# The second output projection in seven products for each pair of token tiles, with the sums on GpSimd

## The reference, cut to what matters

```
mixed = concat([norm(att) * g_att, norm_per_head(mlstm * sigmoid(gate)) * g_ml])   # [1024, 1024]
x     = x1 + mixed @ w_out_2          # second output projection, the product that is changed
q     = (rms_norm(x) * norm_cross_2) @ w_cq_2       # queries of the attention to memory
mem   = rms_norm(mem_2) * norm_mem_2                # its keys and values come from mem
```

## Time and profile before

| what | value |
|---|---|
| median of three runs | 2126.6 us (2122.72 to 2126.88) |
| span of the profiled execution | 2124.1 us |
| PE busy in it | 2037.9 us (96%) |
| DVE, ACT, POOL busy | 915.3, 573.6, 326.1 us |
| first turn of the phase to the `MANY` products of the next projection | 1165.49 to 1300.31 us of the span |
| PE busy in that stretch | 134.48 of 134.82 us |
| DVE, ACT, POOL busy in that stretch | 64.65, 31.86, 8.60 us |

### The profile page before, as it was taken

How to read it: one execution, slowest core, us unless ns; L and a number is a source line. 1 busy time by engine, 2 the same in 40 slices (tenths; PEclk the granted TensorE clock), 3 DMA queues, 4 the chain that set the end, 5 groups by cost and what they waited for, 6 DMA issues and landing times.

```text
span 2124.1 us, 37932 instructions
## 1 busy us (share of the span) xinstructions
PE 2037.9 (96%) x15636; PEld 1158.4 (55%) x15636; DVE 915.3 (43%) x1510; ACT 573.6 (27%) x1048; POOL 326.1 (15%) x292
## 2 busy tenths in 40 slices
PE   6999999999999999999999999999899999999996
PEld 3486655655334445543456444565566666666653
DVE  2535551555556642886466554244611111111114
ACT  2123322333663210442133221143011111111113
POOL 0214430532330012004000010000100000000003
PEclk9999999999999999999999999999899999999999
DMA  8210311123104026100122102100899999999986
GB/s 317 86 45 25 105 60 60 70 85 104 40 8 151 30 90 153 71 1 0 40 80 81 68 0 80 43 31 40 319 384 410 413 410 411 405 403 410 400 359 244
DMA packets 108971, 346.90 MB, mean 163 GB/s; under 512 B 20216, under 2 KB 59536, under 8 KB 95952
## 3 DMA queue, kind: packets, MB, share of 16 engines
q1 hardware_dynamic: 64272, 274.98, 33.3%
q0 software_dynamic: 14528, 48.51, 6.8%
q10 hardware_dynamic: 30080, 22.18, 3.2%
HBM read 310.77 MB, written 40.24 MB: 165 GB/s over the span
## 4 chain that ended last, share of the span: by engine, by line
PE 86%; DVE 7%; ACT 4%; issue 1%; DMA 1%; POOL 1%; DVEq 0%; ACTq 0%; POOLq 0%; PEldq 0%
PE bank L685 19%; PE bank L1482 16%; PE bank L692 11%; PE bank L840 9%; PE bank L1498 8%; ACT work L1602 3%; PE bank L927 2%; PE bank L866 2%; PE bank L1263 1%; PE bank L1059 1%; PE bank L760 1%; PE bank L1488 1%; PE bank L1473 1%; DVE O L2115 1%; PE bank L1064 1%
## 5 line engine op out<-in xcount | busy, mean ns | idle before, releaser
L685 PE MATMUL bank<-slots,HT 128*128 128x512 f32 (+2 forms) x832 | 295.3, 511 | 1.7 <-DVEq L144 1.1
L1602 ACT ACTIVATE work<-bank 128x512 f32<-128x512 f32 (+6 forms) x227 | 117.4, 522 | 406.1 <-PE bank L685 120.0
L685 PEld LDWEIGHTS bank<-slots,HT 128*128 128x128 f32 x832 | 146.4, 190 | 134.0 <-issue 128.7
L1602 ACT ACTIVATE HT<-bank 64x256 f32<-64x256 f32 (+2 forms) x215 | 92.9, 432 | 433.0 <-PE bank L1482 278.4
L1602 ACT ACTIVATE work<-work 128x1024 f32<-128x1024 f32 (+7 forms) x199 | 158.6, 808 | 169.2 <-DVEq L144 114.4
L1482 PE MATMUL bank<-slots,HT 128*32 128x256 f32 x3136 | 172.4, 379 | 2.2 <-DVE HT L2862 1.3
L2868 DVE TENSOR_TENSOR HT<-HT,bank 64x256 f32<-64x256 f32 x97 | 41.0, 423 | 300.3 <-ACT HT L1602 300.3
L1482 PE MATMUL bank<-work,HT 128*32 128x256 f32 x3072 | 168.7, 379 | 0.0
L2982 POOL TENSOR_TENSOR work<-work 128x1024 f32<-128x1024 f32 (+4 forms) x80 | 120.3, 1504 | 240.8 <-DVEq L144 150.6
L1482 PEld LDWEIGHTS bank<-slots,HT 128*32 128x32 f32 x3136 | 103.1, 110 | 68.5 <-issue 2.9
L1482 PEld LDWEIGHTS bank<-work,HT 128*32 128x32 f32 x3072 | 101.1, 110 | 64.6
(11 more groups left out here) (319 smaller groups left out, 2922.5 us busy)
## 6 DMA issues: line engine op xcount, KB each, us to landing
slots<-in_w_e_gate_dram SPq DMA_DIRECT2D x17, 2048.0 KB, 11.1
slots<-in_w_e_up_dram SPq DMA_DIRECT2D x17, 2048.0 KB, 15.8
slots<-in_w_e_down_dram SPq DMA_DIRECT2D x17, 2048.0 KB, 17.2
work<-in_w_e_gate_dram SPq DMA_DIRECT2D x16, 2048.0 KB, 11.4
work<-in_w_e_up_dram SPq DMA_DIRECT2D x16, 2048.0 KB, 15.9
work<-in_w_e_down_dram SPq DMA_DIRECT2D x16, 2048.0 KB
slots<-in_w_in_dram SPq DMA_DIRECT2D x9, 2048.0 KB, 8.4
slots<-in_w_ada_dram SPq DMA_DIRECT2D x6, 2048.0 KB, 14.8
```

The costliest lines, as they stand in the source:

```text
L685: ins = pe.matmul(bank, lhsT, rhs, start=(n == 0), stop=(n == len(pairs) - 1))
L1602: return act.activation(o, i, f, bias=bias, scale=scale, **more)
```

## The change: what it does

The eight tiles are taken as four pairs, `r` = 0 to 3, with tiles `a = 2r` and `b = 2r + 1`. For a pair the product of a 2 by 2 block matrix (two tiles by two halves of the features) with another (two halves of the features by two halves of the columns) is formed in Winograd's variant of Strassen's scheme: seven block products in place of eight. Each is an `of_four` of eight trace records, and they go to three banks: `O2_BY_Q`, `O2_BOTH` and `O2_FAR` (banks 4 to 6).

* POOL forms four sums of weights once, over 4 x 512 = 2048 elements per partition each (`O2_T1`, `O2_T2`, one in place in the slot of `out2_1`, `O2_T4`). It does this at the start of the phase, behind the first two loads of the residual.
* POOL forms four sums of the turned tiles for each pair (`row_sums`, 512 elements per partition each), written over `O` of the same pair.
* ACT copies the first product of a pair out of its bank to `O2_RAW`; POOL adds it to three of the four quarters of the residual of the pair (512 elements each).
* DVE reads the banks six times for each pair in place of four times.
* The residual is loaded pair by pair: pairs 0 and 1 at the start, pair 2 and 3 when the place of pair 0 and 1 is free.
* PE turns tiles 0 and 1 before anything else, then does the last four gate products, and then the pairs.
* `mix_normed(1)` no longer waits for the late gates; `mix_normed(6)` does.
* The weight sums of `cross_q` come behind all of this on POOL, and the load of `mem_2` is issued in the next phase. The slots of `out2_0` and `out2_1` are both given back after the last of the 28 products.

```diff
-        X2 = [cut(work[:, at * T:(at + 2) * T], 2) for at in (10, 12, 14, 6)]
+        X2 = [cut(work[:, at * T:(at + 2) * T], 2) for at in (14, 6, 14, 6)]
+        O2_T1, O2_T2, O2_T4 = (cut(work[:, at * T:(at + 2) * T], 4) for at in (10, 12, 16))
+        O2_BY_Q, O2_BOTH, O2_FAR = banks[4:7]
...
@@ tensor @@
+            ringV.use([banks[7], banks[3], banks[2]])
+            for i in range(2):
+                turn_mixed(i)
             gates_ahead(4)
+            for r in range(NT // 2):
+                a, b = 2 * r, 2 * r + 1
+                (s1, s2), (s4, s3) = O2_ROW_SUMS[r]
+                pe.wait_ge(ringA.free, turned[b])
+                if r:
+                    pe.wait_ge(o2_by_dve, 6 * r - 2)
+                of_four(O2_BY_Q, HT[:, FEW, a * P:(a + 1) * P], w1[:, FEW, :], o2_made, last=False)
+                if r:
+                    turn_back(a - 2)
+                    pe.wait_ge(o2_by_dve, 6 * r)
+                pe.wait_ge(o2_rows, 4 * r + 2)
+                pe.wait_ge(o2_weights, 2)
+                of_four(O2_BOTH, s2, O2_T2, o2_made, last=False)
+                of_four(O2_FAR, s1, O2_T1, o2_made, last=False)
+                if r:
+                    turn_back(b - 2)
+                pe.wait_ge(o2_by_dve, 6 * r + 1)
+                pe.wait_ge(o2_rows, 4 * r + 3)
+                pe.wait_ge(o2_weights, 3)
+                of_four(O2_BOTH, s3, w2[:, FEW, :], o2_made, first=False, last=False)
+                if b + 1 < NT:
+                    turn_mixed(b + 1)
+                pe.wait_ge(o2_raw, r + 1)
+                of_four(O2_BY_Q, HT[:, MANY, a * P:(a + 1) * P], w1[:, MANY, :], o2_made, first=False)
+                pe.wait_ge(o2_by_dve, 6 * r + 3)
+                pe.wait_ge(o2_rows, 4 * r + 4)
+                of_four(O2_FAR, s4, w2[:, MANY, :], o2_made, first=False)
+                if b + 2 < NT:
+                    turn_mixed(b + 2)
+                pe.wait_ge(o2_weights, 4)
+                of_four(O2_BOTH, HT[:, MANY, b * P:(b + 1) * P], O2_T4, o2_made, first=False)
+            chunk_over["out2_0"] = chunk_over["out2_1"] = o2_made, 7 * (NT // 2)
...
+            for i in range(NT - 2, NT):
+                turn_back(i)
...
@@ scalar @@
+            for r in range(NT // 2):
+                act.wait_ge(o2_made, 7 * r + 1)
+                if r:
+                    act.wait_ge(o2_started, 3 * r)
+                line(func(O2_RAW, O2_BY_Q, ACT.Copy), o2_raw)
+                if r + 1 < NT // 2:
+                    for i in range(2 * r + 2, 2 * r + 4):
+                        mix_root(i)
+                    for i in range(2 * r + 2, 2 * r + 4):
+                        turned_tile(i)
+                    tell("pool")
+                for i in range(2 * r, 2 * r + 2):
+                    root_of(i, JUNK2)
...
@@ vector @@
+            for r in range(NT // 2):
+                rows, more = O[:, 2 * r:2 * r + 2, :], r + 1 < NT // 2
+                if r:
+                    turned_tile(2 * r - 2, normcols["norm_cross_2"])
+                if more:
+                    mix_normed(2 * r + 2)
+                out2_added(r, 2, 0, UPPER, O2_BOTH, X2[r], 1)
+                if r:
+                    turned_tile(2 * r - 1, normcols["norm_cross_2"])
+                if more:
+                    mix_normed(2 * r + 3)
+                out2_added(r, 4, 1, UPPER, O2_BOTH, X2[r], 2)
+                out2_added(r, 4, 1, UPPER, O2_FAR, rows)
+                dve.wait_ge(dma_in[r], 48)
+                out2_added(r, 5, 0, LOWER, O2_BY_Q, X2[r])
+                out2_added(r, 6, 0, UPPER, O2_FAR, rows)
+                out2_normed(2 * r)
+                out2_added(r, 7, 1, LOWER, O2_BOTH, X2[r], 3)
+                if more:
+                    tell("pool")
+                out2_normed(2 * r + 1)
...
@@ gpsimd @@
+            for r in range(2):
+                load_residual(r)
+            line(pool.tensor_tensor(O2_T1, w2[:, FEW, :], w1[:, FEW, :], ALU.subtract), o2_weights)
+            line(pool.tensor_tensor(O2_T2, w2[:, MANY, :], O2_T1, ALU.subtract), o2_weights)
+            line(pool.tensor_tensor(w2[:, FEW, :], w2[:, MANY, :], w2[:, FEW, :], ALU.subtract), o2_weights)
+            line(pool.tensor_tensor(O2_T4, w1[:, MANY, :], O2_T2, ALU.subtract), o2_weights)
+            row_sums(0)
+            for r in range(NT // 2):
+                pool.wait_ge(o2_raw, r + 1)
+                pool.wait_ge(dma_in[r], 48)
+                for x, c in ((0, UPPER), (1, UPPER), (1, LOWER)):
+                    to = X2[r][:, x, c]
+                    line(pool.tensor_tensor(to, to, O2_RAW, ALU.add), o2_started)
+                if r + 1 < NT // 2:
+                    row_sums(r + 1)
+                    hear("dve")
+                    if r + 2 < NT // 2:
+                        load_residual(r + 2)
```

More of the change, by code:

```diff
@@ L550, in program @@
         CQ_SUMS = [HT[:, FEW, LOWER], cut(work[:, 8 * T:10 * T], 4), HT[:, FEW, UPPER], HT[:, MANY, LOWER]]
-        CQ_WEIGHT_SUMS = [[cut(work[:, 10 * T + (2 * m + x) * HALF:10 * T + (2 * m + x + 1) * HALF], 4) for x in range(2)]
+        CQ_WEIGHT_SUMS = [[cut(work[:, 14 * T + (2 * m + x) * HALF:14 * T + (2 * m + x + 1) * HALF], 4) for x in range(2)]
                           for m in range(2)]
@@ L1315, in _ @@
             pe.wait_ge(phase, 4 * phases[0])
-            hear("dve")
-            turn_tile(0, O[:, 0, :], ringA)
-            gates_ahead(4)
[L1321 to L1343, removed]
@@ L1344, in _ @@
+            chunk_over["out2_0"] = chunk_over["out2_1"] = o2_made, 7 * (NT // 2)
+            pe.wait_ge(ringA.free, ringA.filled)
+            pe.wait_ge(ringV.free, turned_back[3])
+            weights("cross_q")
+            for m in range(2):
+                of_four(CQ_BOTH[m], cq_weights(FEW, m), HT[:, FEW, LOWER], cq_made, last=False)
+            for i in range(NT - 2, NT):
+                turn_back(i)
             for m in range(2):
@@ L1348, in _ @@
                     pe.wait_ge(ringV.free, ringV.filled)
+                    ringV.use(banks[4:8])
                     phases[0] += 1
@@ L1987, in _ @@
             for i in range(2):
-                do(OT[:, 2 + i, :], M2[:, i, :], ACT.Square, accum_out=ss[:, 8 + i:9 + i])
+                do(MT.rearrange("p a b -> p (a b)")[:, i * D:(i + 1) * D], M2[:, i, :], ACT.Square, accum_out=ss[:, 8 + i:9 + i])
             tell("dve")
@@ L2662, in _, with out2_added, out2_normed @@
                 mix_normed(i)
[L2663 to L2678, removed]
+            def out2_added(r, made, x, c, bank, with_, started=0):
+                dve.wait_ge(o2_made, 7 * r + made)
+                if started:
+                    dve.wait_ge(o2_started, 3 * r + started)
+                line(dve.tensor_tensor(O[:, 2 * r + x, c], bank, with_[:, x, c], ALU.add), o2_by_dve)
+            def out2_normed(i):
+                root(i)
+                ts(NORMED2[i % 2], O[:, i, :], rstd[:, i:i + 1], None, ALU.mult)
+                tell("pe")
+            for r in range(NT // 2):
[17 more added lines that the diff above has]
+                if more:
+                    tell("pool")
+                out2_normed(2 * r + 1)
+            for i in range(NT - 2, NT):
+                turned_tile(i, normcols["norm_cross_2"])
             t1, t2, t3, t4 = CQ_SUMS
@@ L3133, in _, with load_residual @@
             next_phase()
-            for n in range(4):
-                pool.dma_start(X2[n], x1[2 * n:2 * n + 2].rearrange("i p d -> p i d")).then_inc(dma_in[n], 16)
+            def load_residual(r):
+                pool.dma_start(X2[r], x1[2 * r:2 * r + 2].rearrange("i p d -> p i d")).then_inc(dma_in[r], 16)
+            for r in range(2):
+                load_residual(r)
+            for name in ("out2_0", "out2_1"):
+                pool.wait_ge(slot_full[chunk_of[name] % 3], loads_before(name))
@@ new lines, in _, with row_sums @@
+            w1, w2 = slot_of("out2_0"), slot_of("out2_1")
+            line(pool.tensor_tensor(O2_T1, w2[:, FEW, :], w1[:, FEW, :], ALU.subtract), o2_weights)
+            line(pool.tensor_tensor(O2_T2, w2[:, MANY, :], O2_T1, ALU.subtract), o2_weights)
+            line(pool.tensor_tensor(w2[:, FEW, :], w2[:, MANY, :], w2[:, FEW, :], ALU.subtract), o2_weights)
+            line(pool.tensor_tensor(O2_T4, w1[:, MANY, :], O2_T2, ALU.subtract), o2_weights)
+            def row_sums(r):
+                (s1, s2), (s4, s3) = O2_ROW_SUMS[r]
+                a11, a12, a21, a22 = (HT[:, ks, (2 * r + x) * P:(2 * r + x + 1) * P] for x in range(2) for ks in (FEW, MANY))
+                hear("act")
+                line(pool.tensor_tensor(s1, a21, a22, ALU.add), o2_rows)
+                line(pool.tensor_tensor(s2, s1, a11, ALU.subtract), o2_rows)
+                line(pool.tensor_tensor(s3, a11, a21, ALU.subtract), o2_rows)
+                line(pool.tensor_tensor(s4, a12, s2, ALU.subtract), o2_rows)
@@ L3136, in _ @@
             pool.wait_ge(row_in, 64)
[L3137 to L3140, removed]
```

(2 more changed lines are left out.)

37 lines of the change are left out of this document (25 added, 12 removed).

## The result

The changed kernel took 2135.27 us (median of 4 runs, 2134.67 to 2138.47), the kernel before 2126.36 (4 runs, 2122.72 to 2126.88). The ratio is 1.0049 with a 95% interval of 1.0036 to 1.0062: slower by 8.9 us, where plus 10.3 was forecast. The profiled execution took 2135.06 with a span of 2133.2, against a span of 2124.1.

The account below looks back on a forecast made before the run. PE, busy 96% of the span, was taken to bound the kernel. The terms -14.4 + 16.8 + 1.8 + 5.6 + 0.5 = +10.3 us took the median from 2126.6 to about 2137 us, range 2128 to 2143.

Parts of the forecast that it names:

- The products: PE's output products: 56 records a pair instead of 64, and two short gaps gone; -14.4 us.
- The start: First two turns: PE idles 8.2 and 8.6 us while POOL's weight sums and DVE's operations alternate; +16.8 us.
- the far bound: Start of the phase: upper end of its cost, 20 us, if small DVE operations wait for POOL too.
- shared ports: Start of the phase: POOL and DVE share the port at half pace, so the start costs about 7 us.
- The clock: Behind the start's idle time: eight records at 1.2 GHz, counted once; +1.8 us, bounds 0 and 4.
- The middle pairs: Two steps between pairs: PE waits 2.1 us for DVE's read of product 2, then 0.7 more; +5.6 us.
- Pair 0: First pair: its late first product delays the copy, ACT's root and DVE's last operations; +0.5 us, of 0 to 2.
- mem_2: Load issued a phase later: hidden by some 4 us, costing nothing; bounds 0 and 5 us.
- A: Start and middle: POOL's large sums don't shut DVE out; -7.1 us, 2119.5; chance 0.12.
- B: Middle pairs keep PE's pace, start costs as forecast; +4.7 us, 2131.3; chance 0.16.
- C: mem_2 or the row sums come late, 5 us on top; 2142; chance 0.12.

Follow-up runs that it names:

- pieces: Changed kernel with POOL's four 2048-element weight sums each cut into four operations of 512; 2130.65 us, ratio 1.0017 to the kernel before.
- sums_on_dve: Changed kernel with the four weight sums moved from POOL to DVE, behind mix_normed(1); 2124.01 us, ratio 0.9991 to the kernel before.
- gates_inside: Changed kernel with the last four gate products between the turns of tiles 0 and 1; phase 154.15 us, one execution, 2127.85 us.
- fill_in_wait: Changed kernel with four filler records on PE before product 4 of pairs 1 and 2; 2137.11 us, ratio 1.0051.
- adds_of_one_column: Changed kernel with POOL adding the copied bank to one of 512 residual columns; only the phase is read, 152.28 us against 157.30.
- reads_in_front: Changed kernel with DVE's bank reads before the next tiles from pair 1 on, ACT finishing tiles one by one; 2130.58 us, ratio 1.0024.
- early_sums: Changed kernel with gates between turns, reads first, one weight sum on POOL a phase earlier in pieces, three on DVE; 2118.38 us, ratio 0.9964.

## Why the prediction was right

**The products** (-14.4): held, by the records and by their pitch, still 3.43 us for eight. The 288 records from which the 0.7 us of gaps were worked out are 280 (8 of gates, 256, 16 of the next projection); 0.7 follows from 280.

**The start** (+16.8 in waits): 12.70 + 3.69 = 16.4, both counted from where PE would otherwise have gone on (turns at 21.27 and 26.70 of the phase, in place of 8.57 behind the earlier gates). The mechanism was the one laid out: whole operations in turns, DVE's end 0.56 behind POOL's. `pieces` and `sums_on_dve` show it from two sides. The division was off: 8.2 and 8.6 were forecast. I had let the first sum meet no operation of DVE; it held two small ones of 128x1 elements for 4.04 us (0.80 in `pieces`), so all four sums fell into `mix_normed(0)`. That small operations wait too was named as the far bound, but priced at 20 in all, not at 16.4. `mix_normed(0)` ended 4.5 us later than laid out, but `mix_normed(1)` was then free of POOL and was over within 0.4 us of the forecast. The rule of the Trainium skill that I had cited (SBUF — State Buffer, section "SBUF: two separate sides") agrees with these rows; by shared ports the start would have cost 7 us.

**The clock** (+1.8): this is the term that was mis-sized; it came to 6.0. At the start 2.6: two turns 0.9 longer each, and the gates 4.49 for 3.60, with the clock back at 1.00 from 1186 on. The other 3.4 are the records of 5.40 and 5.23 behind the two waits of 2.33 us. I had priced those waits and had asked only of the long ones what they do to the clock. Over all profiles, of ten middle waits of 2.3 us six were followed by slow records (all four in the changed kernel's two profiles, one of two in `pieces` and in `sums_on_dve`, none of two in `gates_inside`), and none of the twelve waits of 0.4 to 0.7 in the middle of `fill_in_wait`, `adds_of_one_column`, `reads_in_front` and `early_sums`. For the filler alone, with its two waits at product 4, luck is not excluded: four of the ten long waits were spared as well.

**The middle pairs** (+5.6): two waits at product 4, each 2.5 us late by the pitch, 5.0; forecast were 2.1 twice, and 0.7 twice at product 6. The latter (0.45 when it came) was hidden by the slow records. The cause was as argued: POOL's adds against the first two operations of `mix_normed` (1.7 us), and reads that stand behind it. The experiments that take one of these away (`adds_of_one_column`, `reads_in_front`) take most of the wait away; 0.66 and 0.65 are left.

**Pair 0** (+0.5): 0.6 (0.43 idle). **`mem_2`** (nothing): ACT's squares of it began at 1324.28 and PE had its turns to do at 1339.74; the load landed 5.3 us after its issue, now that no four loads are issued in front of it, where it had taken 12.8.

The phase's sum is -14.4 + 16.4 + 2.6 + 0.6 + 5.0 + 3.4 = +13.6, where 13.9 was measured and 10.3 forecast. That the total of +8.9 came nearer to the forecast than the phase did is luck: the parts ahead and behind gave 4.8 back, which no step of mine foresaw. Of these, 3.1 are the granted clock and 1.8 PE's idle time, by the estimate above; why they fell is left open. `pieces` has the changed kernel's code ahead of the phase and starts it at 1156.93, so it isn't the change's by itself. With the phase's 13.9 alone the time would have been about 2140, still inside the range of 2128 to 2143.

Of the rivals, A is refused (the start cost 16.4, not 5.4), B too (from product 4 to product 4 it took 30.1 and 31.8 us, the latter with 1.8 of slow records in it, where PE needs 27.5), and C's condition did not occur.

## What to carry to other kernels

What a sum on GpSimd costs a neighbour on VectorE is not told by both engines' busy shares. It hangs on the length of its single operation, on how much of it falls beside VectorE's work, and on whether VectorE is being waited for then. Cutting the weight sums up took 6.5 us off the phase here; taking them off GpSimd took 10.0; moving one of them to an earlier phase left 1.9 us of waits there. Seven products for eight gained here only once the sums' place and the order of the reads were made for it; the products themselves gave 14.4 us, and the first arrangement paid more than that back. Price each new wait of TensorE together with what its clock does afterwards, also one of 2.3 us.

## What I had not expected of the hardware

* An idle time of 2.33 us of PE was followed by a fall of the granted clock to 0.50 (2.4 to 1.2 GHz) while it was at work again: the window 1230:1232 above. It did not always happen, as counted above. The two waits of `pieces` differ by 0.01 us and the eight records behind them by 1.68:

```profile
1225.05 5.38 PE L700 MATMUL bank<-slots,O 128*128 128x512 f32 x8 [2.35 <-DVE O L2721]
...
1256.87 3.70 PE L700 MATMUL bank<-slots,O 128*128 128x512 f32 x8 [2.34 <-DVE O L2721]
```

  What decides between the two no run shows. That short waits leave the clock alone rests on those 12 cases and on six more, of 1.03 to 2.03 us, at the start and in pair 0 of `pieces`, `sums_on_dve`, `gates_inside` and `early_sums`: the filler may have been lucky, as `gates_inside` was.
* Operations of 128x1 elements on DVE are held by POOL as well: two took 4.04 us, where they took 0.36 before, and were over 0.03 us behind POOL's sum.
* DVE's own long operation gets longer too: 2048 elements took 2.29 us alone and 3.24 against POOL's row sums, and those took 3.2 us in place of 1.27.

The timeline of DVE in `early_sums` at that operation, with POOL idle:

```profile
1170.16 2.29 DVE L2718 TENSOR_TENSOR work<-slots 128x2048 f32<-128x2048 f32 x1 [0.25 <-DVE O L2166]
```
